# The output projection of the prompt tokens by Strassen's seven products

## The reference

```python
mixed = jnp.concatenate([o_gla, o_s5], axis=-1).astype(h.dtype)
h = h + mixed @ p['w_out']            # (tokens, 2048) @ (2048, 2048)
hn = rmsnorm(h, p['g_ffn'])
h = h + hier_moe(hn.reshape(-1, D_MODEL), p['w_rg'], p['b_rg'], p['w_re'], p['b_re'],
                 p['w_gate'], p['w_up'], p['w_down']).reshape(h.shape)
```

## Time and profile before

| | us |
|---|---|
| median of 3 runs | 1545.22 (1543.78 to 1546.92) |
| the profiled execution | 1545.47 |
| its span on the core | 1543.7 |
| output projection | 447.7 to 598.9 |
| routing and gather, until the weight loads go on | 598.9 to 627.8 |
| experts | 627.8 to 1543.7 |

### The profile page before, as it was taken

How to read it: one execution, slowest core, us unless ns; L and a number is a source line. 1 busy time by engine, 2 the same in 40 slices (tenths; PEclk the granted TensorE clock), 3 DMA queues, 4 the chain that set the end, 5 groups by cost and what they waited for, 6 DMA issues and landing times.

```text
span 1543.7 us, 18875 instructions
## 1 busy us (share of the span) xinstructions
PE 1336.4 (87%) x7626; PEld 758.2 (49%) x7626; DVE 472.2 (31%) x1003; ACT 260.5 (17%) x684; POOL 84.8 (5%) x249
## 2 busy tenths in 40 slices
PE   7999999999999999889876887876877876886886
PEld 6667777765578886344332342432342342342232
DVE  5387667232530004213202202202202201201334
ACT  4452332353221111030000000000000000000003
POOL 7800000100010002000000000000000000000000
PEclk9999999999999999998998897988987988986998
DMA  9332233261369763799999999999999999999997
GB/s 220 113 110 92 72 110 97 71 169 55 110 239 380 269 215 108 303 428 428 427 428 428 429 428 429 429 428 428 428 428 428 428 428 428 429 428 428 427 425 316
DMA packets 113173, 480.97 MB, mean 312 GB/s; under 512 B 17873, under 2 KB 85781, under 8 KB 86149
## 3 DMA queue, kind: packets, MB, share of 16 engines
q1 hardware_dynamic: 111496, 475.71, 77.1%
q0 software_dynamic: 1328, 4.37, 1.0%
q10 hardware_dynamic: 288, 0.04, 0.0%
HBM read 470.03 MB, written 10.78 MB: 311 GB/s over the span
## 4 chain that ended last, share of the span: by engine, by line
PE 51%; DMA 44%; DVE 2%; issue 1%; SPq 1%; ACT 1%; POOLq 0%; POOL 0%; ACTq 0%; DVEq 0%
DMA arena<-in_w_up 44%; PE ps L2155 20%; PE ps L2419 12%; PE ps L2219 7%; PE ps L2223 2%; PE ps L2090 1%; PE ps L2469 1%; PE ps L2025 1%; PE ps L2013 1%; SPq L565 1%; PE ps L2077 1%; DVE arena L1552 0%; DMA arena<-in_x_prompt 0%; PE ps L2329 0%; PE ps L2023 0%
## 5 line engine op out<-in xcount | busy, mean ns | idle before, releaser
L2419 PE MATMUL ps<-arena 128*32 128x512 f32 x2048 | 302.6, 743 | 140.5 <-DMA arena<-in_w_up 140.0
L2155 PE MATMUL ps<-arena 128*128 128x336 f32 (+1 forms) x1152 | 328.3, 442 | 0.0
L2155 PEld LDWEIGHTS ps<-arena 128*128 128x128 f32 x1152 | 215.3, 190 | 95.9 <-issue 3.7
L2419 PEld LDWEIGHTS ps<-arena 128*32 128x32 f32 x2048 | 80.9, 131 | 333.7 <-issue 332.3
L2469 PE MATMUL ps<-arena 128*32 128x512 f32 x1024 | 142.4, 705 | 19.5 <-DVE arena L1787 19.1
L1777 DVE COPY arena<-ps 128x512 f32<-128x512 f32 x31 | 21.4, 692 | 418.4 <-PE ps L2419 418.4
L2265 PE MATMUL ps<-arena 128*128 128x128 f32 (+1 forms) x672 | 123.5, 314 | 0.0
L1188 ACT ACTIVATE arena<-ps 128x128 f32<-128x128 f32 x32 | 8.8, 276 | 641.7 <-PE ps L2447 641.7
L2265 PEld LDWEIGHTS ps<-arena 128*128 128x128 f32 (+1 forms) x672 | 93.8, 193 | 47.4 <-issue 24.6
L2219 PE MATMUL ps<-arena 128*128 128x256 f32 x512 | 114.4, 382 | 0.0
L2219 PEld LDWEIGHTS ps<-arena 128*128 128x128 f32 x512 | 96.0, 190 | 14.1 <-issue 1.2
(11 more groups left out here) (399 smaller groups left out, 988.2 us busy)
## 6 DMA issues: line engine op xcount, KB each, us to landing
arena<-in_w_down SPq DMA_DIRECT2D x61, 2048.0 KB, 23.2
arena<-in_w_gate SPq DMA_DIRECT2D x59, 2048.0 KB, 19.0
arena<-in_w_up SPq DMA_DIRECT2D x59, 2048.0 KB, 23.5
arena<-in_w_in SPq DMA_DIRECT2D x15, 2048.0 KB, 9.5
arena<-in_w_out SPq DMA_DIRECT2D x8, 2048.0 KB, 8.5
arena<-in_w_up SPq DMA_DIRECT2D x10, 1024.0 KB, 15.1
arena<-in_w_gate SPq DMA_DIRECT2D x10, 1024.0 KB, 13.0
arena<-in_w_down SPq DMA_DIRECT2D x6, 1024.0 KB, 20.8
```

The source lines that it names most:

```text
L2155: mm = te.matmul(o, w, x, start=(k == 0), stop=(k == kt - 1))
L2419: mm = te.matmul(ps[CAP * x:CAP * x + CAP, 0, :], xt[:, 4 * q + at, CAP * i:CAP * i + CAP], (next_first[up] if late and q == 0 else wpiece ...
```

## The change

For a block of 256 columns the prompt part of the product has 256 tokens, 2048 rows of w_out and 256 columns. The change halves all three: two token tiles (t), two halves of the 2048 rows (c), two halves of 128 columns. `MA[t][c]` is the quarter of `mixT`, `quarters(i)[c][h]` that of w_out. In place of eight half-size products there are seven, of 8 matmuls of 128 x 128 x 128 each (`product`). Their operands are quarters or sums of them: `XS1`, `XS2`, `XS4` and a `MA[1][0]` written over, made once by VectorE (`token_sums`), and `WS13`, `WS2`, `WS4`, made for every block (`weight_sums`), where WS13 is used twice (`third_sum` writes it again when its first product is done).

TensorE's order in a block is now: three products into bank 0, the samples, transposes and logits of the block before, then four products into bank 1, each behind a wait for its sum. VectorE's is: first additions from bank 0, samples, the third weight sum, the second additions from bank 1, the first sums of the next block. `wout_done` counts 4 for each block; `h_added` stays at 3, the samples first. Where the sums lie, weights were loaded before: so piece 11 of expert 0 is now loaded behind the last block, and two further quarters of expert 1's w_down too, with the last quarter behind them. ScalarE squares in the new order, and one semaphore (`rows_ready`) is merged into another.

```diff
@@ -255,6 +255,11 @@
+        r = Region(arena, at_d + 6144, 4096)
+        WS4, WS13, WS2, XS1 = (r.take(8, 128) for _ in range(4))
+        r = Region(arena, 22528, 2048)
+        XS2, XS4 = r.take(8, 128), r.take(8, 128)
+        MA = [[mixT[:, 8 * c:8 * c + 8, 128 * t:128 * t + 128] for c in range(2)] for t in range(2)]
         r = Region(arena, at_x, ARENA - at_x)
...
@@ -441,12 +446,16 @@
         XB = (2, 3, 5, 6)
-        OB = ((0, 1, 4), (5, 6, 4))
         FB = (5, 7)
...
         (LR, LI, LDT, DT, X, TH, N_, R_, T1, T2, CARG, MAG, SI, CO, ABR, ABI, DEN, RDEN, FR, FI) = range(20)
+        def quarters(i):
+            w = ring[CIDX[("out", i)] % 2].rearrange("p (k n) -> p k n", n=256)
+            return [[w[:, 8 * c:8 * c + 8, 128 * h:128 * h + 128] for h in range(2)] for c in range(2)]
...
@@ -484,7 +493,7 @@
                     if k0 == "out":
-                        sp.wait_ge(wout_done, 3 * (i0 + 1))
+                        sp.wait_ge(wout_done, 4 * (i0 + 1))
                     else:
...
@@ -575,33 +584,33 @@
                 cols = slice(256 * c, 256 * c + 256)
-                sp.wait_ge(h_added, 3 * c + 2)
+                sp.wait_ge(h_added, 3 * c + 1)
+                sp.dma_start(hn_rows[SEQ:TO, cols], hrow[0:NS, 2, cols]).then_inc(hn_stored, 16)
+                sp.wait_ge(h_added, 3 * c + 3)
                 sp.dma_start(hn_rows[0:SEQ, cols].rearrange("(t p) d -> p t d", p=128), hrow[:, 0:2, cols]).then_inc(hn_stored, 16)
-                sp.wait_ge(h_added, 3 * c + 3)
-                sp.dma_start(hn_rows[SEQ:TO, cols], hrow[0:NS, 2, cols]).then_inc(hn_stored, 16)
...
                     sp.wait_ge(states_stored, 32)
-                if i < 5:
+                if i < 4:
                     expert_weights(0, None, range(4 * i - 8, 4 * i - 4))
+                if i == 4:
+                    expert_weights(0, None, [8, 9])
+                    expert_weights(0, None, [10], True)
                 if i == 6:
...
                     sp.wait_ge(wr_ready, 2)
-                    sp.wait_ge(piece_loaded[8], 16)
                     sp.wait_ge(piece_loaded[10], 16)
                     down = A["w_down"][0, 1].rearrange("(p k) n -> p (k n)", k=4)
-                    sp.dma_start(arena[:, at_d + 6144:at_d + 6144 + 4096], down[:, 0:4096]).then_inc(piece_loaded[8], 16)
                     sp.dma_start(next_down[2], down[:, 4096:6144]).then_inc(piece_loaded[10], 16)
...
             store_rows(7)
-            sp.wait_ge(wout_done, 24)
-            sp.dma_start(next_down[3], A["w_down"][0, 1].rearrange("(p k) n -> p (k n)", k=4)[:, 6144:8192])\
-                .then_inc(piece_loaded[11], 16)
+            sp.wait_ge(wout_done, 32)
+            expert_weights(0, None, [11], True)
             sp.wait_ge(piece_loaded[2], 16)
...
@@ -610,6 +619,10 @@
                 .then_inc(piece_loaded[0], 16)
+            sp.wait_ge(piece_loaded[8], 16)
+            sp.dma_start(arena[:, at_d + 6144:at_d + 6144 + 4096], down[:, 0:4096]).then_inc(piece_loaded[8], 16)
+            sp.wait_ge(piece_loaded[11], 16)
+            sp.dma_start(next_down[3], down[:, 6144:8192]).then_inc(piece_loaded[11], 16)
             expert_weights(1, 1, [1, 3, 4, 6, 5, 7], True)
...
@@ -1154,10 +1167,10 @@
             for i in range(8):
-                for t in range(3):
-                    act.wait_ge(h_added, 3 * i + t + 1)
-                    if 3 * i + t:
-                        act.wait_ge(h_ss, 3 * i + t)
+                for j, t in enumerate((2, 0, 1)):
+                    act.wait_ge(h_added, 3 * i + j + 1)
+                    if 3 * i + j:
+                        act.wait_ge(h_ss, 3 * i + j)
                     sc.activation(hjunk[0:TR[t]], hrow[0:TR[t], t, 256 * i:256 * i + 256], ACT.Square,
...
@@ -1585,18 +1598,79 @@
+            def token_sums():
+                dve.wait_ge(mix_gla, 2 * (NCH - 1))
+                dve.wait_ge(mix_s5, 8)
+                st(ve.tensor_tensor(XS1, MA[1][0], MA[1][1], ALU.add))
+                st.sync()
+                st(ve.tensor_tensor(XS2, XS1, MA[0][0], ALU.subtract))
+                st.sync()
+                ve.tensor_tensor(XS4, MA[0][1], XS2, ALU.subtract).then_inc(sums_ready, 1)
+                st(ve.tensor_tensor(MA[1][0], MA[0][0], MA[1][0], ALU.subtract))
+            def weight_sums(i):
+                n, w = CIDX[("out", i)], quarters(i)
+                dve.wait_ge(ring_loaded[n % 2], 16 * (n // 2 + 1))
+                ve.tensor_tensor(WS13, w[0][1], w[0][0], ALU.subtract).then_inc(sums_ready, 1)
+                dve.wait_ge(sums_ready, 4 * i + 2)
+                ve.tensor_tensor(WS2, w[1][1], WS13, ALU.subtract).then_inc(sums_ready, 1)
+                if i == 0:
+                    dve.wait_ge(s_stored, 16)
+                dve.wait_ge(sums_ready, 4 * i + 3)
+                ve.tensor_tensor(WS4, w[1][0], WS2, ALU.subtract).then_inc(sums_ready, 1)
+            def third_sum(i):
+                w = quarters(i)
+                dve.wait_ge(wout_done, 4 * i + 3)
+                ve.tensor_tensor(WS13, w[1][1], w[0][1], ALU.subtract).then_inc(sums_ready, 1)
+            def hq(i):
+                return hrow[:, 0:2, 256 * i:256 * i + 256].rearrange("p t (h c) -> p t h c", h=2)
+            def add_first(i):
+                h = hq(i)
+                dve.wait_ge(wout_done, 4 * i + 1)
+                st(ve.tensor_tensor(h, h, ps[:, 0, 0:128].unsqueeze(1).unsqueeze(1).broadcast_to([128, 2, 2, 128]), ALU.add))
+                st.sync()
+                st(ve.tensor_tensor(h[:, 0], h[:, 0], ps[:, 0, 128:384].rearrange("p (h c) -> p h c", h=2), ALU.add))
+            def add_samples(i):
+                dve.wait_ge(wout_done, 4 * i + 2)
+                d_ = hrow[0:NS, 2, 256 * i:256 * i + 128]
+                st(ve.tensor_tensor(d_, d_, ps[0:NS, 4, 0:128], ALU.add))
+                d_ = hrow[0:NS, 2, 256 * i + 128:256 * i + 256]
+                ve.tensor_tensor(d_, d_, ps[NS:2 * NS, 4, 0:128], ALU.add).then_inc(h_added, 1)
+            def add_second(i):
+                h = hq(i)
+                P5, P6, P4, P7 = (ps[:, 1, 128 * x:128 * x + 128] for x in range(4))
+                dve.wait_ge(wout_done, 4 * i + 4)
+                st.sync()
+                st(ve.tensor_tensor(h[:, 0, 1], h[:, 0, 1], P6, ALU.add))
+                st(ve.tensor_tensor(h[:, 1], h[:, 1], bc(P6.unsqueeze(1), 1, 2), ALU.add))
+                st.sync()
+                ve.tensor_tensor(h[:, :, 1], h[:, :, 1], bc(P5.unsqueeze(1), 1, 2), ALU.add).then_inc(h_added, 1)
+                dve.wait_ge(h_added, 3 * i + 2)
+                st(ve.tensor_tensor(h[:, 1], h[:, 1], bc(P7.unsqueeze(1), 1, 2), ALU.add))
+                st.sync()
+                ve.tensor_tensor(h[:, 1, 0], h[:, 1, 0], P4, ALU.add).then_inc(h_added, 1)
+            token_sums()
+            weight_sums(0)
             dve.wait_ge(res_loaded, 48)
             for i in range(8):
-                for t in range(3):
-                    dve.wait_ge(wout_done, 3 * i + t + 1)
-                    if t < 2:
-                        d_ = hrow[:, t, 256 * i:256 * i + 256]
-                        ve.tensor_tensor(d_, d_, ps[:, OB[i % 2][t], 0:256], ALU.add).then_inc(h_added, 1)
-                    else:
-                        d_ = hrow[0:NS, t, 256 * i:256 * i + 128]
-                        st(ve.tensor_tensor(d_, d_, ps[0:NS, OB[i % 2][t], 0:128], ALU.add))
-                        d_ = hrow[0:NS, t, 256 * i + 128:256 * i + 256]
-                        ve.tensor_tensor(d_, d_, ps[NS:2 * NS, OB[i % 2][t], 0:128], ALU.add).then_inc(h_added, 1)
+                add_first(i)
+                add_samples(i)
+                third_sum(i)
+                add_second(i)
+                if i < 7:
+                    weight_sums(i + 1)
             ve.memset(xrow0, 0.0).then_inc(xrow_cleared, 1)
...
@@ -2184,12 +2258,11 @@
                     pe.wait_ge(hl_copied, 2)
-                pe.wait_ge(h_added, 3 * i + 2)
+                pe.wait_ge(h_added, 3 * i + 3)
                 for k in range(2):
...
                                      hrow[:, t, 256 * i + 128 * k:256 * i + 128 * k + 128], ident)
-                pe.wait_ge(h_added, 3 * i + 3)
                 for k in range(2):
...
@@ -2203,30 +2276,42 @@
+            def product(bank, x, left, right):
+                for m in range(8):
+                    mm = te.matmul(ps[:, bank, 128 * x:128 * x + 128], left[:, m], right[:, m], start=(m == 0), stop=(m == 7))
+                return mm
             pe.wait_ge(mix_s5, 8)
...
                 w = ring[n % 2].rearrange("p (k n) -> p k n", n=256)
-                for t in range(3):
-                    if t == 2 and i:
-                        pe.wait_ge(h_added, 3 * i)
-                    elif i >= 2:
-                        pe.wait_ge(h_added, 3 * (i - 2) + t + 1)
-                    for m in range(16):
-                        if t < 2:
```

(34 more changed lines are left out.)

18 lines of the change are left out of this document (9 added, 9 removed).

## The result

The changed kernel takes 1563.77 us (1562.26 to 1564.42) beside 1546.04 of the kernel before: a ratio of 1.0113, with an interval of 1.0099 to 1.0128. By this ratio it is 17.5 us slower. The forecast was 1555.2, with a range that ended at 1562. The sign and the main place were right, the size was not.

A forecast was written before the change was run, and what follows sets the result against it. TensorE was taken to bound the projection, a serial chain the routing, and DMA the last 915.9 us. +10.9 - 3.3 + 1.7 + 0.7 = +10.0 us gave 1555.2 against the median of 1545.22; range 1549.5 to 1562.

The forecast's parts named there:

- The seven products' rate: TensorE in the projection: 112 instructions of 128 columns at 0.112 us each, 12.5 us a block, weight loads hidden.
- The two rivals about it: Projection: each product's start costs 0.1 to 0.19 us, 1560 to 1564 (0.12); or weight loads don't hide, 1643 (0.03).
- the rule that the prediction weighed from the Trainium skill: TensorE weight loads overlap matmuls in flight only when the row group differs; pitch 0.21 us, block 23.9 us.
- The period: Projection from the second block on: 18.6 us a block, 0.47 less than before; seven blocks give back 3.3 us.
- The stall of block 0: TensorE idles 9.6 us before block 0's last product, for the third sum behind VectorE's residual-row wait; block 0 +10.9 in all.
- The half clock behind it: After block 0's idle time, the last product takes 3.6 us instead of 1.8, plus 0.5 for what follows.
- the +7.6: End of the projection: moves by +10.9 from block 0 less 3.3 from the seven later blocks.
- The end of the projection: Behind the last product: transposes wait 2.05 us for additions, ScalarE's copies follow 0.84 later; +1.7 us.
- The moved transfers and the gather: Behind the projection: 6 MB last until 20.5 us after its end and slow the gather by 0 to 2 us; +0.7 taken.
- Rival 1: Block 0: the residual rows are no obstacle, usable by 459.6; 1543.0 us, no measurable change or slightly faster; chance 0.09.
- The last stretch: Expert weights to the end: fixed bytes at 422 GB/s, 915.9 us that move with their start and keep their length.
- The sum: Whole kernel: +10.9 - 3.3 + 1.7 + 0.7 = +10.0 us.

The follow-up runs named there:

- later logits: Changed kernel with TensorE computing the logits of the block before behind product (1,0) instead of directly behind the transposes: 1557.29 us, ratio 1.0073.
- dummies in the gap: Changed kernel with 16 dummy matmuls of 320 columns in TensorE's 10.4 us gap of block 0: 1560.1 us, ratio 1.0093.
- With dummies there: Changed kernel with two dummy matmuls of 512 columns on TensorE ahead of the transposes of block 7: 1564.24 us, ratio 1.0109.
- with them put right: Changed kernel: third sum earlier, logits and state stores later, three quarters behind the gather, block 7's samples last, expert 0's pieces a block later: 1541.94 us, 0.9966.

## Why the prediction was wrong

- **The seven products' rate: right.** The two rivals about it fell. 48 instructions take 5.55 us with the last one's drain, and 112 take 12.70 in the chain: 0.113 each, where 0.112 was taken. A start behind a satisfied wait costs nothing that shows, and the weight loads of 128 rows hide. This goes against the rule that the prediction weighed from the Trainium skill (TensorE: Matmul & The Clock Gate, Part 3, The mechanism). The same section also says that a load for the background weight buffer is pulled ahead of matmuls in flight, which the prediction left out and which agrees with the 0.113 us.
- **The period: right in kind, 0.22 us too short.** The step was the logits: 0.67 us from their start to the next product's (492.04 to 492.71 in the timeline with later logits) and 1.74 from the first transpose to them, where 0.57 and 1.66 were read. Seven blocks, 1.5 us.
- **The stall of block 0: right in place, cause and end.** Predicted 9.6 us, measured 10.4, with the third sum ending it. That it had a second door (block 1's first product waits for the samples' addition) was not said. It would have mattered for the repair: moving the sum alone gained 4 us, not 13.
- **The half clock behind it: about right.** It was given 1.8 + 0.5 us, for the last product and a little more. The clock was at half for 6 us of TensorE's work, and that cost 2.85 in this profile (dummies in the gap) and 1.5 to 1.8 in the three others with such a gap. Stall, clock and period together make 2.9 of the 3.1 us by which the projection's +10.7 is above the +7.6.
- **The end of the projection: the mechanism was right, the clock was put at nothing.** The transposes began 2.0 us late, as forecast; the following steps then ran at half clock in this profile (1.57 for two dummies against 0.84), +3.2 instead of +1.7. Where the clock stayed up it was +1.8 (16.9 in the ledger).
- **The moved transfers and the gather: this is the step that failed.** The 6 MB were taken to be through 20.5 us after the projection's end, and the gather was costed as a fair share of the DMA engines up to there: 0.7 us, with a bound of 2. Measured were 2.4 in the gather, up to 3.5 when it was asked for earlier, and 4.2 in the whole when the loads alone were moved (kernel before with moved loads, 2.6 to 5.9). Two things were wrong. First, the end of the transfers: the last quarter landed 25.4 us after the end. The sum took 422 GB/s behind a lag of 3.0 us, but from 613 to 636 us, with the gather's own rows among them, the engines moved 326 GB/s. The lag was read short as well, since before the change the last of the 3 MB landed 11.4 us after the first issue (611.5 - 600.1), not 10.5. Second, the share: with the block open until 25.4 us the gather was not slowed for a part of its time, it landed when the block did. With the predicted 20.5 even that rule would have cost nothing, as the gather would have ended later anyway (16.7 + 5.87 = 22.6).
- **The range: too narrow at the top.** Its upper bound held 2 us for half clock, 1.3 more for the gather and 3 for starts. The starts cost nothing, and nothing was held for half clock behind the projection's end, for the period or for anything behind the gather.
- **A rival's argument.** Rival 1 put the residual rows at 1.5 MB and 3.7 us. The three requests are 1, 1 and 0.5 MB, 2.5 MB, and 6.2 us at the 422 GB/s used there. That rival fell in any case: the rows landed 16.3 us after the last request. The 23.9 us of the weighed rule should be 112 x 0.21 = 23.5, which changes nothing.
- **The last stretch: right.** From before to the changed kernel it keeps its length within 0.3 us; everything ahead of it moves the end one for one. The 1.1 us ahead of the projection and the 0.8 behind the gather lie within what these steps scatter, though part of the 0.8 may be the moved loads'.
- **The sum.** +10.0 was forecast, +17.5 measured in the medians. In the profiles: 3.1 missed in the projection, 1.5 in the steps ahead of the gather, 1.7 in the gather, and 2.2 in parts that scatter.

What stays open: whether TensorE's clock falls in the 2 us ahead of the last transposes is not the same in every profile, so its share of the median isn't known. With dummies there no gain could be measured while the 6 MB hold the gather. The scatter of the half clock behind the gap (1.5 to 2.85 us) is not explained either. And each stage's share is read from one profile of the changed kernel, whose miss is 8.6 us where that of the medians is 7.5.

## What to carry to other kernels

An operation that is put into an engine's queue behind an existing wait inherits that wait: look for each wait on each engine's queue that used to be free, and ask which new consumer now stands behind it. Fewer multiplications are worth only what the period shows (here 1 us in 19), so three side effects (the wait in block 0, the additions that stand bare behind the last product, the moved loads) were enough to turn the gain into a loss; with them put right the seven products do win, 0.9966 of the time before. The other edits of that kernel were not tried on the kernel before by themselves, but its projection had no idle time that they could have taken away. Here the gather, which shares its engines with a block of other transfers, had to be costed by when the whole block ends, and that end from the rate of such a stretch, not from the best rate in the trace.
